# A two-block network in fp32: products without a reader in TensorE's waits, a split gather ahead of the experts, and merged slices in the nets

## The chip, the core and the metric

The kernel runs on one NeuronCore of a Trainium2 chip. Its engines are TensorE (PE; PEld is its weight load), VectorE (DVE), ScalarE (ACT), GpSimd (POOL) and SyncE (SP), which issues most of the DMAs. The metric is the device time of one run in microseconds: the kernel before took 2341.85 us, the median of three runs.

## The reference, cut to what matters

Two blocks follow each other on 256 tokens of width 1024, all in fp32. The first ends in an expert layer in which each of 16 experts takes the 32 tokens with the highest router affinity. The second has two layers, each with two feed-forward nets ("nets" below) of hidden width 2816 around a mixing part.

```python
def expert_choice_moe(h, w_router, w_gate, w_up, w_down):
    affinity = jax.nn.softmax((h @ w_router).astype(jnp.float32), axis=-1)
    gates, idx = lax.top_k(jnp.swapaxes(affinity, 1, 2), cap)      # cap = 32, 16 experts
    xe = h[b_idx, flat_idx].reshape(B, E, cap, D)
    a = jnp.einsum('becd,edf->becf', xe, w_gate)                   # f = 2048
    u = jnp.einsum('becd,edf->becf', xe, w_up)
    ye = jnp.einsum('becf,efd->becd', jax.nn.silu(a) * u, w_down) * gates[..., None]
    return jnp.zeros_like(h).at[b_idx, flat_idx].add(...)

def swiglu_ffn(x, wi, wo):                                         # two per layer, two layers
    g, u = jnp.split(x @ wi, 2, axis=-1)
    return (jax.nn.silu(g) * u) @ wo
```

## The kernel before, in words

Each engine has its own program, and semaphores order them. VectorE and ScalarE finish one operation before the next begins, through the helper in which every one of their instructions is recorded (line 208).

**Split products.** Outside the experts, fp32 values are multiplied in rounded halves. A weight unit (128 rows of 1024 values) is copied rounded by ScalarE (the high part) and its remainder is written by VectorE (the low part). `split_mm` then makes three products into the same PSUM place: high by high, high by low, low by high (line 1910 for the layers, 1624 for the first block). Four unit buffers go round; SyncE fills a ring of six 1 MB slots with weights ahead of them.

**A net** has 22 steps. In step c TensorE makes `up(c + 1)`, which is a gate unit and an up unit of 8 row slices each, and then `down(c)`, which is 12 products of 512 columns. VectorE and ScalarE make the hidden slice of c in between: VectorE multiplies gate and up sums out of PSUM, ScalarE takes the tanh, and VectorE writes the high and low part of the slice (`hid_split`) and splits the next units (`sub`). A loop of five turns holds four steps each, and two steps follow it.

**The experts** stream 192 pieces of 2 MB through eight buffers: three pairs of ring slots, `wide`, three of `moe_ring` and `turned_and_rows`. Piece i goes to buffer i mod 8. SyncE issues the pieces in order, each when its buffer has been used (`big_fill`), and waits besides, for the first eight, until the buffer's earlier contents are dead. An expert uses eight pieces for gate and up and four for down. Experts run in a loop of four groups of four.

**Ahead of the first expert** stands a chain. The output projection ends the mixing part of the first block. POOL meanwhile writes a row of modulation values (`mod_rows`) to DRAM and reads it back broadcast to all partitions; VectorE needs it for the residual and the new norm. TensorE transposes the two token tiles, multiplies them by the router matrix (the logits), transposes the probabilities, and VectorE selects 32 tokens an expert with four rounds of a maximum of eight. One-hot rows are made, and the gather is 32 products of 512 columns for all sixteen experts into all eight PSUM banks; eight copies, eight transposes and the opening of the output sums follow before the first expert's product.

## Time and profile before

| | us |
|---|---|
| median of 3 runs | 2341.85 |
| the runs | 2339.44 to 2343.32 |
| the profiled execution | 2342.55 |
| its span, first to last instruction | 2340.8 |

| engine | busy us | share of the span | instructions |
|---|---|---|---|
| PE | 1896.8 | 81% | 12667 |
| PEld | 1345.1 | 57% | 12667 |
| DVE | 969.1 | 41% | 1348 |
| ACT | 696.4 | 30% | 963 |
| POOL | 42.7 | 2% | 68 |

The DMA engines moved 660.73 MB. The shares are means over stages with different limits: the first block up to some 226 us, the experts up to some 1143 us, and the two layers of the second block behind them. A stage's limit is read from its own rows.

### The profile page before, as it was taken

How to read it: one execution, taken by the hardware profiler on the slowest of the kernel's cores; microseconds unless marked ns; L12 is line 12 of the kernel's file. 1: busy time of each engine (PE TensorE's matmuls, PEld its weight loads, DVE VectorE, ACT ScalarE, POOL GpSimd, SP SyncE). 2: the span in 40 equal slices, each digit the busy share in tenths (PEclk: the TensorE clock that was granted, in tenths of full speed). 3: DMA queues.
4: the chain of work that ended last, by engine and by line, in shares of the span. 5: the costliest groups of instructions: out<-in, count | busy, mean ns of one | idle time of the engine just before them, and what ended most of it. 6: DMA issues, size and time to landing. Idle time of an engine off the chain costs nothing.

```text
span 2340.8 us, 33186 instructions
## 1 busy us (share of the span) xinstructions
PE 1896.8 (81%) x12667; PEld 1345.1 (57%) x12667; DVE 969.1 (41%) x1348; ACT 696.4 (30%) x963; POOL 42.7 (2%) x68
## 2 busy tenths in 40 slices
PE   6896655656555556566699999999999999999999
PEld 4674111111111111111499987799989998879997
DVE  3474000000000000000366677676767667766665
ACT  4342000000000000000344455444454435644444
POOL 0000000000000000000000010000000001000000
PEclk8997787787787777877899999999999999999999
DMA  9767999999999999999846653445546475344552
GB/s 366 247 257 310 429 429 428 428 428 428 428 428 429 428 428 428 428 429 428 303 162 204 219 180 127 162 144 188 188 144 198 163 246 176 127 140 164 182 185 85
DMA packets 174812, 660.73 MB, mean 282 GB/s; under 512 B 10051, under 2 KB 108140, under 8 KB 143732
## 3 DMA queue, kind: packets, MB, share of 16 engines
q1 hardware_dynamic: 171980, 654.12, 72.3%
q10 hardware_dynamic: 2376, 3.03, 0.6%
q0 software_dynamic: 352, 2.11, 0.2%
q8 instruction: 75, 1.23, 0.2%
q14 instruction: 29, 0.24, 0.0%
HBM read 656.60 MB, written 2.64 MB: 282 GB/s over the span
## 4 chain that ended last, share of the span: by engine, by line
PE 53%; DMA 37%; DVE 6%; ACT 2%; issue 2%; ACTq 0%; DVEq 0%; POOL 0%; PEldq 0%; POOLq 0%; SPq 0%; PEld 0%
PE PS L1910 43%; DMA turned_and_rows<-in_w_down_e 12%; DMA turned_and_rows<-in_w_gate_e 12%; DMA turned_and_rows<-in_w_up_e 11%; PE PS L1872 3%; DVE arena L208 2%; DVE units L208 2%; PE PS L1624 2%; DVE hn L208 1%; DMA ring<-in_w_in 1%; PE PS L1892 1%; ACT units L208 1%; DMA ring<-in_w_ada 1%; PE PS L2036 1%; PE PS L1593 0%
## 5 line engine op out<-in xcount | busy, mean ns | idle before, releaser
L208 ACT ACTIVATE units<-ring 128x1024 fp32r<-128x1024 f32 (+2 forms) x416 | 438.1, 1053 | 473.3 <-PE PS L1910 425.7
L208 DVE TENSOR_TENSOR units<-ring,units 128x1024 fp32r<-128x1024 f32 (+2 forms) x416 | 505.8, 1216 | 167.9 <-ACT units L208 140.0
L1910 PE MATMUL PS<-hT_split,units 128*128 128x256 f32 x4416 | 545.4, 283 | 1.7 <-DVE hT_split L208 1.7
L1910 PEld LDWEIGHTS PS<-hT_split,units 128*128 128x128 f32 x4416 | 541.1, 192 | 9.8 <-issue 2.6
L208 DVE SCALAR_TENSOR_TENSOR arena<-arena,PS 128x512 f32<-128x512 f32 (+1 forms) x54 | 41.4, 767 | 798.8 <-ACT arena L208 518.0
L208 ACT ACTIVATE arena<-PS 32x256 f32<-32x256 f32 (+4 forms) x135 | 66.9, 496 | 926.8 <-PE PS L1880 310.6
L1910 PE MATMUL PS<-units,hT_split 128*128 128x512 f32 (+2 forms) x1248 | 286.6, 388 | 5.3 <-DVE units L208 2.8
L1910 PEld LDWEIGHTS PS<-units,hT_split 128*128 128x128 f32 x1248 | 231.6, 190 | 50.6 <-DVE units L208 4.9
L1910 PE MATMUL PS<-units,hid_split 128*128 128x512 f32 x1056 | 255.5, 391 | 0.0
L1910 PEld LDWEIGHTS PS<-units,hid_split 128*128 128x128 f32 x1056 | 192.9, 188 | 36.7
L1872 PE MATMUL PS<-moe_ring,arena 128*32 128x512 f32 x768 | 129.4, 808 | 93.3 <-DMA moe_ring<-in_w_gate_e 55.0
L1872 PE MATMUL PS<-ring,arena 128*32 128x512 f32 x768 | 129.6, 810 | 88.9 <-DMA ring<-in_w_up_e 51.3
L1872 PEld LDWEIGHTS PS<-moe_ring,arena 128*32 128x32 f32 x768 | 25.0, 129 | 193.5 <-DMA moe_ring<-in_w_up_e 69.6
L1872 PEld LDWEIGHTS PS<-ring,arena 128*32 128x32 f32 x768 | 24.9, 130 | 190.1 <-DMA ring<-in_w_up_e 82.4
L1892 PE MATMUL PS<-moe_ring,arena 128*32 128x256 f32 x768 | 72.0, 539 | 37.5 <-DMA moe_ring<-in_w_down_e 34.0
L1892 PE MATMUL PS<-ring,arena 128*32 128x256 f32 x768 | 63.5, 488 | 39.7 <-DMA ring<-in_w_down_e 39.7
L208 ACT ACTIVATE arena<-arena 128x256 f32<-128x256 f32 (+3 forms) x133 | 58.4, 439 | 111.9 <-DVE arena L208 103.2
L208 DVE TENSOR_TENSOR arena<-PS,hn 128x256 f32<-128x256 f32 (+1 forms) x90 | 39.8, 442 | 94.6 <-PE PS L1910 89.8
L1872 PE MATMUL PS<-turned_and_rows,arena 128*32 128x512 f32 x256 | 46.9, 870 | 34.8 <-DMA turned_and_rows<-in_w_gate_e 19.1
L1892 PEld LDWEIGHTS PS<-moe_ring,arena 128*32 128x32 f32 x768 | 30.4, 145 | 75.3 <-DMA moe_ring<-in_w_down_e 41.1
L1872 PE MATMUL PS<-wide,arena 128*32 128x512 f32 x256 | 43.1, 806 | 35.4 <-DMA wide<-in_w_up_e 15.3
L1892 PEld LDWEIGHTS PS<-ring,arena 128*32 128x32 f32 x768 | 27.6, 135 | 76.8 <-DMA ring<-in_w_down_e 55.3
(206 smaller groups left out, 1229.4 us busy)
## 6 DMA issues: line engine op xcount, KB each, us to landing
ring<-in_ffn_wi SPq DMA_DIRECT2D x88, 1024.0 KB, 5.5
ring<-in_w_gate_e SPq DMA_DIRECT2D x24, 2048.0 KB, 36.1
moe_ring<-in_w_up_e SPq DMA_DIRECT2D x24, 2048.0 KB, 35.6
ring<-in_w_down_e SPq DMA_DIRECT2D x24, 2048.0 KB, 35.5
moe_ring<-in_w_gate_e SPq DMA_DIRECT2D x24, 2048.0 KB, 35.5
ring<-in_w_up_e SPq DMA_DIRECT2D x24, 2048.0 KB, 37.0
moe_ring<-in_w_down_e SPq DMA_DIRECT2D x24, 2048.0 KB, 36.9
ring<-in_ffn_wo SPq DMA_DIRECT2D x44, 1024.0 KB, 5.0
```

Of the source, the lines that this page charges most:

```text
L208: return instruction(*args, **kwargs)
L1624: passes = [mm(out, lhs[i], rhs[j], start=start and i + j == 0, stop=stop and i == 1, **flags) for i, j in ((0, 0), (0, 1), (1, 0))]
L1872: last = mm(PS[32 * g:32 * g + 32, 2 + part, :], xe[:, k, :], big(at, 2, SLOT)[:, kk, 512 * g:512 * g + 512], start=(k == 0), stop=(k == K ...
L1892: last = mm(PS[32 * g:32 * g + 32, 5, 0:256], e_hT[:, s, 32 * j:32 * j + 32], big(at, 4, D)[:, s, 256 * g:256 * g + 256], start=(j == 0 an ...
L1910: passes = [mm(out, lhs[i], rhs[j], start=start and i + j == 0, stop=stop and i == 1, **flags) for i, j in ((0, 0), (0, 1), (1, 0))]
L2036: last = mm(PS[:, bank, :], pT[:, j, t * P:(t + 1) * P], w_ple[:, j, 512 * n:512 * n + 512], start=(j == 0), stop=(j == 1))
```

## The change

1. **Products without a reader.** `keep_busy(bank, n)` makes n fp32 products of 128 x 256 into a PSUM bank that nobody reads. They stand before a dozen of TensorE's waits: around the router's transposes and logits, before the selection's transposes, in each group's last expert, and before transposes of the second block.
2. **The gather in two parts.** The one-hot rows and the gather are made for the first four experts first (32 products of 128 columns); VectorE copies the first expert's rows straight out of PSUM, and the first expert begins. The rest (32 products of 384 columns, the copies, the transposes, the opening of the sums) stands between that expert's up and down products. The first group of experts is therefore written out ahead of the loop.
3. **Buffers renumbered.** Pieces 0 to 2 go to the ring pairs and piece 3 to `wide`. The first three pieces wait for ring slots alone.
4. **Selection and copies.** The first maximum reads PSUM, one subtraction is gone (the constant counts from 1), and ScalarE copies the whole first tile's transposes before it squares the second.
5. **Merged slices in the nets.** In 19 of the 22 steps the first two products of a row slice, which share their weights, become one product of 512 columns over both parts of the moving side. The two column halves of the PSUM bank have to be added: VectorE does it with a reduction over pairs. Gate and up take a bank each. Steps 0, 1 and 21 stay as they were, and the loop has four turns.
6. **Order in the mixing parts.** Single operations of VectorE, ScalarE and TensorE are moved against each other.

TensorE between the output projection and the first expert, before (L1815 are the transposes, L1822 the logits, L1827 and L1831 the selection's transposes, L1840 the gather, L1848 and L1853 what follows it):

```order
L1815 MATMUL PS<-cst,hn 128x128 x8
L1822 MATMUL PS<-arena,hT 128x16 x8
L1815 MATMUL PS<-cst,hn 128x128 x8
L1822 MATMUL PS<-arena,hT 128x16 x8
L1827 MATMUL PS<-cst,arena 16x128 x2
L1831 MATMUL PS<-cst,arena 128x16 x2
L1840 MATMUL PS<-onehot_rounded,hn_split 128x512 x32
L1848 MATMUL PS<-cst,arena 128x128 x8
L1853 MATMUL PS<-zeros 128x2 x4
```

And in the change, where L1643 is `keep_busy`, L1880 and L1888 are transposes and logits, L1900 and L1905 the selection's transposes, L1916 the gather and L1968 the expert:

```order
L1643 MATMUL PS<-cst 128x256 x2
L1888 MATMUL PS<-arena,hT 128x16 x8
L1643 MATMUL PS<-cst 128x256 x3
L1880 MATMUL PS<-cst,hn 128x128 x8
L1643 MATMUL PS<-cst 128x256
L1888 MATMUL PS<-arena,hT 128x16 x8
L1643 MATMUL PS<-cst 128x256 x4
L1900 MATMUL PS<-cst,arena 16x128 x2
L1643 MATMUL PS<-cst 128x256 x11
L1905 MATMUL PS<-cst,arena 128x16 x2
L1643 MATMUL PS<-cst 128x256
L1916 MATMUL PS<-onehot_rounded,hn_split 128x128 x32
```

The gather has shrunk from 512 to 128 columns, and L1643 stands before each wait. Behind these rows come 64 products of the first expert, and only then the other part of the gather (128x384 x32).

VectorE in one step of a net, before (`hn` is the row of roots, the `TENSOR_TENSOR units` rows are splits of weight units):

```order
L208 TENSOR_TENSOR arena<-PS,hn 128x256
L208 TENSOR_TENSOR arena<-arena,PS 128x256
L203 REGISTER_ALU
L208 TENSOR_TENSOR units<-ring,units 128x1024
L203 REGISTER_ALU
L208 SCALAR_TENSOR_TENSOR arena<-arena 128x256
L208 CAST hid_split<-arena 128x256
L208 TENSOR_TENSOR hid_split<-arena,hid_split 128x256
L203 REGISTER_ALU
L208 TENSOR_TENSOR units<-ring,units 128x1024
```

And in the change:

```order
L210 TENSOR_REDUCE arena<-PS 128x256
L210 TENSOR_TENSOR arena<-arena,hn 128x256
L205 REGISTER_ALU
L210 TENSOR_TENSOR units<-ring,units 128x1024
L210 TENSOR_REDUCE arena<-PS 128x256
L210 TENSOR_TENSOR arena<-arena 128x256
L205 REGISTER_ALU
L210 SCALAR_TENSOR_TENSOR arena<-arena 128x256
L210 CAST hid_split<-arena 128x256
L210 TENSOR_TENSOR hid_split<-arena,hid_split 128x256
L205 REGISTER_ALU
L210 TENSOR_TENSOR units<-ring,units 128x1024
```

Each of the two products out of PSUM has become a reduction out of PSUM and a product in SBUF, with the down unit's split between the gate and the up half.

VectorE at the branch products of a layer, before (`head_ms` marks the normed rows of one branch, `a_split` its second part, 128x16 the attention's sink):

```order
L208 TENSOR_TENSOR arena<-arena,head_ms 128x1024
L208 TENSOR_TENSOR arena<-arena 128x1024
L208 TENSOR_TENSOR units<-ring,units 128x1024
L208 SCALAR_TENSOR_TENSOR hn<-PS,wide 128x256
L208 SCALAR_TENSOR_TENSOR hn<-PS,wide 128x128
L208 TENSOR_REDUCE arena<-hn 128x1 x2
L208 TENSOR_SCALAR arena<-arena,cur 128x2
L208 TENSOR_TENSOR arena<-arena,cur 128x16
L208 TENSOR_TENSOR a_split<-PS,a_split 128x1024
L208 TENSOR_TENSOR units<-ring,units 128x1024 x4
```

VectorE at the same place in the change:

```order
L210 SCALAR_TENSOR_TENSOR hn<-PS,wide 128x256
L210 SCALAR_TENSOR_TENSOR hn<-PS,wide 128x128
L210 TENSOR_REDUCE arena<-hn 128x1 x2
L210 TENSOR_SCALAR arena<-arena,cur 128x2
L210 TENSOR_TENSOR arena<-arena,head_ms 128x1024
L210 TENSOR_TENSOR arena<-arena 128x1024
L210 TENSOR_TENSOR units<-ring,units 128x1024
L210 TENSOR_TENSOR arena<-arena,cur 128x16
L210 TENSOR_TENSOR units<-ring,units 128x1024 x2
L210 TENSOR_TENSOR a_split<-PS,a_split 128x1024
L210 TENSOR_TENSOR units<-ring,units 128x1024 x2
```

The last head's scores (the rows on `hn<-PS,wide` to 128x2) stand before the normed rows now, and two of the four unit splits before `a_split`.

The diff, cut to its core:

```diff
-            return (POS_LAYER + 2 * (m - 1)) % R
+            return (POS_LAYER + 2 * m) % R

         def big(i, *dims):

             m = i % BIG
-            if m == 0:
+            if m < 3:
+                v = ring[:, ring_pair(m):ring_pair(m) + 2, :].rearrange("p a n -> p (a n)")
+            elif m == 3:
                 v = wide.rearrange("p a n -> p (a n)")
-            elif m < 4:
-                v = ring[:, ring_pair(m):ring_pair(m) + 2, :].rearrange("p a n -> p (a n)")
             elif m < 7:
                 v = moe_ring[:, m - 4, :]
             else:
...
-                if i == 0:
+                if i < 3:
+                    sp.wait_ge(S["slot_used"], POS_LAYER - R + 2 * i + 2)
+                elif i == 3:
                     sp.wait_ge(S["x_mid"], 1)
-                elif i < 4:
-                    sp.wait_ge(S["slot_used"], POS_LAYER - R + 2 * (i - 1) + 2)
                 elif i == 4:
                     sp.wait_ge(S["mixed"], NT)
...
+                if t == 1:
+                    act.wait_ge(S["first_T"], 7)
+                    activation(hT[:, :, 0:P], two_banks(4).rearrange("p (k n) -> p k n", k=KT), ACT.Copy).then_inc(
+                        S["first_hT"], 1)
...
             dve.wait_ge(S["select_T"], 1)
-            dve.run(V.tensor_copy, affT[0:NE, :], PS[0:NE, 1, 0:TOK])
             for i in range(CAP // 8):
-                dve.run(V.max, top8[0:NE, :], affT[0:NE, :])
-                dve.run(V.match_replace, affT[0:NE, :], top8[0:NE, :], affT[0:NE, :], -1.0)
+                left = PS[0:NE, 1, 0:TOK] if i == 0 else affT[0:NE, :]
+                dve.run(V.max, top8[0:NE, :], left)
+                dve.run(V.match_replace, affT[0:NE, :], top8[0:NE, :], left, -1.0)
             ts(chosen[0:NE, :], affT[0:NE, :], -1.0, None, ALU.is_equal)
             dve.run(V.tensor_tensor_scan, count[0:NE, :], chosen[0:NE, :], zeros[0:NE, :], 0.0, ALU.add, ALU.add)
-            tt(count[0:NE, :], count[0:NE, :], chosen[0:NE, :], ALU.mult)
-            ts(affT[0:NE, :], count[0:NE, :], 1.0, None, ALU.subtract).then_inc(S["selected"], 1)
+            tt(affT[0:NE, :], count[0:NE, :], chosen[0:NE, :], ALU.mult).then_inc(S["selected"], 1)
             dve.wait_ge(S["select_T"], 2)
-            for t in range(NT):
-                last = tt(onehot_rounded[:, t, :, :], con("cap_iota").unsqueeze(1).to_broadcast([P, NE, CAP]),
-                   wide_of(PS[:, 2, t * NE:t * NE + NE], CAP), ALU.is_equal)
-            last.then_inc(S["selected"], 1)
+            for first, last_e in ((0, GROUP), (GROUP, NE)):
+                for t in range(NT):
+                    last = tt(onehot_rounded[:, t, first:last_e, :],
+                              con("cap_iota").unsqueeze(1).to_broadcast([P, last_e - first, CAP]),
+                              wide_of(PS[:, 2, t * NE + first:t * NE + last_e], CAP), ALU.is_equal)
+                last.then_inc(S["selected"], 1)
+            for half in range(2):
+                dve.wait_ge(S["gathered"], half + 1)
+                last = dve.run(V.tensor_copy, xe[:, 4 * half:4 * half + 4, :],
+                               PS[:, 6 + half, :].rearrange("p (k n) -> p k n", k=4)[:, :, 0:CAP])
+            last.then_inc(S["xe"], 1)
...
-                def sub(c, hidden, base):
-                    act_, gu = f_act[:, c % 2, :], f_gu[:, c % 2, :]
-                    if c == FFN_SUBS - 1:
-                        down_rest(off, c, base)
-                    dve.wait_ge(S["unit_used"], base + (2 * off + gate_unit(c) + 2))
-                    tt(act_, PS[:, c % 4, 0:TOK], root_row, ALU.mult).then_inc(S["f_gate"], 1)
-                    tt(gu, act_, PS[:, c % 4, TOK:2 * TOK], ALU.mult)
-                    if c < FFN_SUBS - 1:
-                        down_rest(off, c, base)
...
+                    act_, gu = f_act[:, c % 2, :], f_gu[:, c % 2, :]
+                    if c == FFN_SUBS - 1:
+                        down_rest(off, c, base)
+                    gate_bank, up_bank = 2 * (c % 2), 2 * (c % 2) + 1
+                    if c in SPLIT_SUBS:
+                        dve.wait_ge(S["unit_used"], base + (2 * off + gate_unit(c) + 2))
+                        tt(act_, PS[:, gate_bank, 0:TOK], root_row, ALU.mult).then_inc(S["f_gate"], 1)
+                        tt(gu, act_, PS[:, gate_bank, TOK:2 * TOK], ALU.mult)
+                        if c < FFN_SUBS - 1:
+                            down_rest(off, c, base)
+                    else:
+                        dve.wait_ge(S["unit_used"], base + (2 * off + gate_unit(c) + 1))
+                        dve.run(V.reduce_sum, act_, PS[:, gate_bank, :].rearrange("p (i n) -> p n i", i=2), AX.X)
+                        tt(act_, act_, root_row, ALU.mult).then_inc(S["f_gate"], 1)
+                        down_rest(off, c, base)
+                        dve.wait_ge(S["unit_used"], base + (2 * off + gate_unit(c) + 2))
+                        dve.run(V.reduce_sum, gu, PS[:, up_bank, :].rearrange("p (i n) -> p n i", i=2), AX.X)
+                        tt(gu, act_, gu, ALU.mult)
...
+                piece_rest(5, 2, 3)
                 sw_scores(0)
-                piece_rest(5, 2, 3)
...
+                sw_scores(7)
                 dve.wait_ge(S["head_roots"], l + 2)
                 tt(h_a, h_a, wide_of(by_head(head_ms[:, :]), ML_DV), ALU.mult)
                 tt(sq, sq, mo, ALU.mult).then_inc(S["branch"], 1)
                 piece_rest(8, 3, 4)
-
-                sw_scores(7)
                 tt(sw_stat[:, 2, :, :], sw_stat[:, 0, :, :], wide_of(p_("sink"), NT), ALU.add).then_inc(
                     S["sink_arg"], 1)
+                halves_rest(stage_units(OFF_WA, 2, 0, 2), D, before)
                 dve.wait_ge(S["branch_hi"], 2 * l + 1)
                 tt(a_split[:, 1, :, :].rearrange("p k n -> p (k n)"), PS[:, 4:6, :].rearrange("p b n -> p (b n)"),
                    a_split[:, 0, :, :].rearrange("p k n -> p (k n)").bitcast(F32), ALU.subtract).then_inc(
                     S["branch_hT"], 1)
-                halves_rest(stage_units(OFF_WA, 2), D, before)
+                halves_rest(stage_units(OFF_WA, 2, 2), D, before)
...
+                if name == "mixed":
+                    keep_busy(2, 3)
...
+            def keep_busy(bank, n):
+
+                for _ in range(n):
+                    mm(PS[:, bank, 0:TOK], ident, con("causal")[:, 0:TOK], start=True, stop=True)
...
-            for t in range(NT):
+            def moe_turn(t):
+
+                if t == 0:
+                    pe.wait_ge(S["const_full"], 48)
+                    pe.wait_ge(S["x_mid"], 2)
+                    keep_busy(1, 4)
+                else:
+                    keep_busy(1, 3)
                 pe.wait_ge(S["h_moe"], t + 1)
...
+            logits(1).then_inc(S["logits"], 1)
+            keep_busy(3, 4)
             pe.wait_ge(S["selected"], 1)
...
+            keep_busy(3, 11)
             pe.wait_ge(S["selected"], 2)
...
+            keep_busy(3, 1)
...
-                        last = mm(PS[:, k, :], hn_split[:, i, t, k:D:KT],
-                                  onehot_rounded[:, t, :, :].rearrange("p e c -> p (e c)"),
+                        last = mm(out, hn_split[:, i, t, k:D:KT],
+                                  onehot_rounded[:, t, first:last_e, :].rearrange("p e c -> p (e c)"),
                                   start=(t + i == 0), stop=(t + i == NT))
+                return last
+
+            for half in range(2):
+                for k in range(4):
+                    last = gather(PS[:, 6 + half, k * P:(k + 1) * P], 4 * half + k, 0, GROUP)
                 last.then_inc(S["gathered"], 1)
-            pe.wait_ge(S["xeT"], KT)
-            pe.wait_ge(S["selected"], 4)
-            for q in range(NQ):
-                for t in range(NT):
-                    last = nc.tensor.transpose(
-                        PS[:, 4 + q // 2, (q % 2) * TOK + t * P:(q % 2) * TOK + (t + 1) * P],
-                        gated[:, t, GROUP * q:GROUP * q + GROUP, :].rearrange("p e c -> p (e c)"), ident)
-            last.then_inc(S["gathered"], 1)
-            for bank in (0, 1, 6, 7):
-                mm(PS[:, bank, 0:2], zeros[0:1, 0:P], zeros[0:1, 0:2], start=True, stop=False, skip_group_check=True)
...
+            def gather_rest():
+
+                pe.wait_ge(S["selected"], 4)
+                pe.wait_ge(S["xeT"], 1)
+                for k in range(KT):
+                    if k == 4:
+                        pe.wait_ge(S["xeT"], 1 + 4)
+                    gather(PS[:, LATE_BANK[k % 4], 0:NE * CAP - P], k, GROUP, NE).then_inc(S["gathered"], 1)
...
                 fills = q * (GROUP_SLOTS // BIG * 16)
+                alone = isinstance(q, int)
...
+                    if alone and r == 0:
+                        gather_rest()
...
+            experts(0)
+            with pe.Fori(1, NQ) as q:
+                experts(q)
...
-                                first, last = split_mm(PS[:, c % 4, part * TOK:(part + 1) * TOK],
-                                                       [unit(i, n, KT, P)[:, k, :] for i in range(2)],
-                                                       [hT_split[:, i, k, :] for i in range(2)],
-                                                       start=(k == 0), stop=(k == KT - 1))
+                                w = [unit(i, n, KT, P)[:, k, :] for i in range(2)]
+                                if c in SPLIT_SUBS:
+                                    first, last = split_mm(PS[:, 2 * (c % 2), part * TOK:(part + 1) * TOK], w,
+                                                           [hT_split[:, i, k, :] for i in range(2)],
+                                                           start=(k == 0), stop=(k == KT - 1))
+                                else:
+                                    bank = 2 * (c % 2) + part
+                                    first = mm(PS[:, bank, :].rearrange("p (i n) -> p i n", i=2), w[0], hT_split[:, :, k, :],
+                                               start=(k == 0), stop=False, skip_group_check=True)
+                                    last = mm(PS[:, bank, 0:TOK], w[1], hT_split[:, 0, k, :], start=False,
+                                              stop=(k == KT - 1), skip_group_check=True)
...
-                        gate_units(0, 1, 3)
-                        neg_m()
+                        gate_units(0, 1, 2)
+                        neg_m(0)
+                        gate_units(0, 2, 3)
+                        neg_m(1)
```

## Rows read from the trace of the kernel before

**Rows 1.** The span in 40 slices, share of the DMA engines (the page, part 2)

```profile
DMA  9767999999999999999846653445546475344552
```

**Rows 2.** Chain of waits in order of time: start us, us, engine, line, count

```profile
225.94 15.52 PE PS L1872 x128
...
1103.49 35.52 DMA turned_and_rows<-in_w_down_e
...
1162.10 181.44 PE PS L1910 x1272
...
1345.25 1.77 PE PS L1566 x16
...
1348.73 11.51 PE PS L1910 x96
...
1413.08 1.92 PE PS L2129 x8
```

**Rows 3.** Timeline of SyncE's DMA issues: start us, us, line, tensors

```profile
177.27 0.37 SPq L511 DMA_DIRECT2D wide<-in_w_gate_e  x1
...
200.74 0.33 SPq L511 DMA_DIRECT2D turned_and_rows<-in_w_up_e  x1
229.46 0.33 SPq L511 DMA_DIRECT2D wide<-in_w_down_e  x1
```

**Rows 4.** By stretch: busy us of each engine, granted TensorE clock, DMA share, GB/s

```profile
196.00:200.00 4.00, 3.22 (x16) 3.03 (x15) 3.14 (x3) 1.66 (x2) 0.00 (x0) 0.50 1.01 430
```

**Rows 5.** DMA issues of 118 to 140 us: size, us to landing

```profile
arena<-mod_rows POOLq DMA_DIRECT2D x1, 1024.0 KB, 9.2
mod_rows<-wide POOLq DMA_DIRECT2D x1, 8.0 KB, 5.6
```

**Rows 6.** DMA issues of 160 to 200 us: size, us to landing

```profile
arena<-mod_rows POOLq DMA_DIRECT2D x1, 1024.0 KB, 5.0
arena<-in_w_router ACTq DMA_DIRECT2D x1, 64.0 KB, 9.7
mod_rows<-wide POOLq DMA_DIRECT2D x1, 8.0 KB, 1.8
```

**Rows 7.** Timeline from the output projection to the first expert

```profile
164.20 0.64 POOL L617 DMA_DIRECT2D mod_rows<-wide  x1 [13.71 <-DVE wide L208]
...
170.52 2.54 DVE L208 TENSOR_TENSOR units<-ring,units 128x1024 fp32r<-128x1024 f32 x2 [0.20 <-ACT units L208]
...
177.32 1.23 DVE L208 TENSOR_TENSOR hn<-PS,arena 128x1024 f32<-128x1024 f32 x1 [0.34 <-ACT arena L208]
...
196.97 3.60 PE L1822 MATMUL PS<-arena,hT 128*128 128x16 f32 x16 [0.78 <-DVE hT L208]
...
203.32 0.42 DVE L208 MAX8 arena<-arena 16x8 f32<-16x256 f32 x1
...
211.44 9.77 PE L1840 MATMUL PS<-onehot_rounded,hn_split 128*128 128x512 f32 x32 [1.63 <-DVE onehot_rounded L208]
```

**Rows 8.** Timeline of one step of a feed-forward net

```profile
1252.88 2.91 PE L1910 MATMUL PS<-units,hid_split 128*128 128x512 f32 x12
...
1253.08 0.42 DVE L208 TENSOR_TENSOR arena<-PS,hn 128x256 f32<-128x256 f32 x1 [0.56 <-PE PS L1910]
1253.60 0.42 DVE L208 TENSOR_TENSOR arena<-arena,PS 128x256 f32<-128x256 f32 x1
...
1255.63 5.92 PE L1910 MATMUL PS<-hT_split,units 128*128 128x256 f32 x48
...
1257.02 1.22 DVE L208 TENSOR_TENSOR units<-ring,units 128x1024 fp32r<-128x1024 f32 x1 [0.16 <-ACT units L208]
```

**Rows 9.** Groups of instructions by form: busy us, mean ns

```profile
L208 DVE TENSOR_REDUCE arena<-arena 128x2 f32<-128x512 f32 x8 | 5.5, 686 | 0.6
```

**Rows 10.** Timeline at the first layer's branch products, VectorE

```profile
1466.73 1.22 DVE L208 TENSOR_TENSOR a_split<-PS,a_split 128x1024 fp32r<-128x1024 f32 x1 [4.41 <-ACT a_split L208]
```

**Rows 11.** The same stretch, TensorE

```profile
1469.42 5.96 PE L1910 MATMUL PS<-units,a_split 128*128 128x512 f32 x24 [1.83 <-DVE units L208]
```

147 lines of the change are left out of this document (97 added, 50 removed).

## The prediction

> **What bounds the kernel now.** I read the page's slices first, then the chain of waits, then timelines of the places that the change touches. The slices show the DMA engines full from the fifth of the 40 to the nineteenth [rows 1]: that is the expert stage. The chain of waits says the same: from 241 to 1139 us it is loads of expert weights, with TensorE only as links between them; the last lands at 1103.49 + 35.52 = 1139.01 us [rows 2]. SyncE reloads a weight buffer for the first time at 229.46 us [rows 3], and 184 of the 192 loads are still to come then: (1139.01 - 229.46) / 184 = 4.943 us each. So the stage ends 909.55 us after the first reload, whatever TensorE does in it, and only an earlier first reload shortens it. Behind it TensorE bounds: a net is one unbroken piece of 1272 products in 181.44 us [rows 2]. Between two nets VectorE and TensorE alternate, with short waits.
>
> **The nets (12.6 us less).** In before, each row slice of the gate and up products is three products of 256 columns; the change makes it one of 512 and one of 256 for 19 of a net's 22 steps. 96 products of 256 columns take 11.51 us, 119.9 ns each [rows 2]; 12 of 512 columns take 1255.63 - 1252.88 = 2.75 us, 229.2 ns each [rows 8]. Check on the whole piece: 1008 x 119.9 + 264 x 229.2 = 181.4 us, as the row has it. A slice then costs 349.1 instead of 359.7 ns, 10.6 less; I take 10.4, with 119.8 out of the step itself. There are 16 slices x 19 steps x 4 nets = 1216, so 12.6 us. From below: no row has a product whose moving side is two separate pieces; if it costs what its two halves cost, the gain is 0.
> The Trainium skill, "TensorE: Matmul & The Clock Gate", section "Back-to-back issue gap", gives N / 2.4 + 2.5 ns for a warm product. By it a merged slice would save only 2.5 ns, 3.0 us in all. The trace disagrees: 119.9 and 229.2 ns are 13 and 16 ns above N / 2.4, so I keep the rows.
> What hides the edit is VectorE, and it gets tight. A merged step takes one reduction of 512 inputs and one product of 256 for each half. The nearest row for a reduction is 686 ns [rows 9], a 256-wide operation is 0.42 us and the split of a weight unit 1.22 [rows 8]. A step then has 2 x 0.69 + 2 x 0.42 + 1.14 (the three that finish the hidden slice) + 3 x 1.23 = 7.05 us in ten operations, with gaps of 0.1 to 0.16 us between them [rows 8], 1.3 in all: 8.35 us. TensorE's step falls from 8.50 to 8.33 us. So the engines are level. A hidden slice is asked for 5.6 us after the last down product ended, and by this count is ready at 2.4, so there are some 3.2 us to use up over 19 steps: a lag of 0.02 us a step does not reach TensorE. The bound upwards: a reduction that costs 1.23 us (what 1024 elements cost) makes the step 9.43 us, a rival below.
>
> **The way to the first expert (9.5 us earlier).** Three terms.
> First, the loads that now come early. Three ring buffers come first in the new numbering and wait only for ring slots, so the first two go out at some 158.4 and 162.9 us, the third at 174.7, instead of all behind the load into wide at 177.27 [rows 3]. The first two, 4 MB, are then in flight when POOL writes its row at 164.20 [rows 7] and reads it back as 1 MB. On free engines these took 1.8 and 5.0 us [rows 6]; the same pair under loads took 5.6 and 9.2 us [rows 5]. So the write lands at 169.8, and the read, issued 0.3 later and clear of the second load from 172.5 on, at 175 to 178; I take 176.6. VectorE is busy with weight splits until 173.06 [rows 7], then wants the read. Its three following operations had 0.3 us to spare before the one at 177.32, which had waited 0.34 us for ScalarE. That is 3.5 - 0.3 = 3.2 us later for everything behind, between 0.5 and 8 (both transfers at the loaded price).
> The Trainium skill, "DMA: Bandwidth & Descriptors", section "Queues, rings and completion order", says that each DMA engine goes round its queue rows packet by packet. By that a write of 8 KB should lose almost nothing, and the term would be near 1 us. The row shows it 3.8 us later under load, so I keep the larger price.
> Second, the router logits. They end at 196.97 + 3.60 = 200.57 us [rows 7]. ScalarE now copies the first tile's transposes before it squares the second tile, so the first logits need not wait until 190.8. But they need the router matrix, 9.7 us after its issue at 179.95 [rows 6], so not before 189.65; 2 of the added products, each 1.92 / 4 = 0.48 us at the full clock [rows 2] and twice that at half, stand behind that wait and 3 more ahead of the second tile's transposes. The logits themselves took 3.60 us at the granted clock of 0.50 [rows 4, 7] and would take 1.8 at 1.00. The end comes between 6.7 us earlier (matrix early, clock full) and 3.5 later (matrix late, clock at half). I take 1 us earlier, near the late case because the row is for a matrix behind loads, as it will be again.
> Third, from the logits to the first reload: 229.46 - 200.57 = 28.9 us now. New, at the full clock: 1.6 to the probabilities and 0.3 for their transposes; the selection 202.8 to 209.4, 6.5 us, less a copy of 0.42 + 0.07 and a subtraction of 0.36, so 5.7; 0.4 for the next transposes; 0.8 for the one-hot rows of four experts instead of sixteen; 32 products of 128 columns at the price of a transpose, 1.77 / 16 = 0.11, so 3.6 us where 32 of 512 took 9.77 and eight copies, eight transposes and the sums followed; 0.6 for the copy of two small pieces; 1.7 for the first buffer's 16 products, (15.52 - 3.5) / 7 [rows 2], instead of 3.5. Sum 14.7, with semaphores 15.2. The 11 added products of 5.3 us just fit in the 5.7 of the selection, and the 4 before (1.9) stick out by 0.3. At the half clock they take 10.6 and 3.8, and all the rest of TensorE's doubles: 26.7 us. I take 17.2, since TensorE is now busy nearly all along but starts from 0.50, so 11.7 us less.
> Sum: 3.2 - 1 - 11.7 = 9.5 us earlier, between 19 earlier and 2 later.
> What was left out of the way, the gather for the other twelve experts (32 products of 384 columns, about 5.7 us, eight transposes, eight copies), now stands between the first expert's up and down products. Behind it wait the down products, and for them the buffers: the first reload begins after 1.7 us of the first expert, eight take 39.5, and the down products begin about 26 us after the start. So the queue never runs dry, and it costs nothing. The 2 products before late loads in each group's last expert sit in waits of 3 us for a load. The 4 ahead of the last sum are 1.9 us against ScalarE's 1.7: 0.2 later.
>
> **The branches of a layer (3.4 us less).** VectorE waited 4.41 us and then wrote the branch's second part before the weight units; TensorE stood 1.83 us for a unit [rows 10, 11]. Now two units come first, inside that wait, and the last head's scores come earlier, which takes 0.6 us off a wait. The third and fourth unit then come last, so of 2.4 us I count 1.3, and 0.4 for the score piece moved behind a unit: 1.7 a layer, twice. Bounds 0 and 5.
> Heads and units reordered in the first block move nothing: TensorE had its half of the units, and the moved exponentials are wanted 10 us later.
>
> **Sum.** The profiled execution took 2342.55 us (span 2340.8). 2342.55 - 12.6 - 9.5 - 3.4 + 0.2 = 2317.3; the median of the runs, 2341.85, is 0.7 lower, so 2316.5 us, 1.1% less.
>
> **Rivals.**
> 1. The way to the expert gains nothing: the added products run at the half clock, hold up logits and selection, and the broadcast comes late. For: TensorE was granted 0.50 in 196 to 200 us though it worked 3.22 of 4 us [rows 4]. Against: in before it then stood idle. 2316.5 + 9.5 = 2326 us.
> 2. The way is clear: matrix early, full clock, broadcast on time: 19 earlier, 2307 us. For: the first big loads are fewer when the router matrix is asked for. Against: both loaded prices of rows 5.
> 3. VectorE becomes the bound in the nets, the slower side. Place: the two reductions out of PSUM, whose two inputs stand 256 columns apart. Price: at 1.23 us each 19 x (9.43 - 8.33) - 3.2 = 17.7 us a net against the forecast, 71 in all: 2387 us. A net gains nothing from about 0.85 us a reduction, the kernel gets slower from about 0.95. For: no row has a reduction of pairs. Against: 512 and 1024 elements cost the same per element in every form shown.
> 4. The merge saves nothing, products of 512 in two pieces costing 2 x 119.8: 2329 us. By the figure of the Trainium skill cited above it would be 2326.
>
> **How the numbers follow.** Forecast 0.57 (2310 to 2323); rival 1 0.17; rival 2 0.10; rival 3 0.09, of which 0.07 is beyond no change; rival 4 0.07. The range 2303 to 2331 us holds the forecast, rivals 1, 2 and 4 and leaves out rival 3 and tails. About 0.2% is what a measurement of this kernel can tell from none: faster 0.88, within it 0.05, slower 0.07.
>
> **What would show it.** Right: 96 slices' products and 24 down products alternate without idle time of TensorE, a net's piece of about 178.3 us instead of 181.4; VectorE's reductions at 0.69 us; the first reload at 216 to 224 us; the last load 909 to 910 us later; the wait at the branch products at most 0.6 us. Wrong: TensorE waiting for hid_split inside a net (rival 3); a granted clock of 0.5 in the selection (rival 1); mod_rows landing before 173 us; a gap in the DMA share between the first reload and the end of the experts, which would mean that the late gather does hold the buffers.

## Result: 2323.9 us, 0.8% faster, 7.4 us short of the forecast

The changed kernel took 2323.91 us (median of 4 runs, 2320.16 to 2325.17) beside 2342.11 us of the kernel before on the same chip (4 runs): ratio 0.9921, 95% interval 0.9904 to 0.9938. It is faster, inside the forecast's range, but 0.9 us above the 2310 to 2323 us of its likeliest case. The profiled execution took 2324.62 us, its span is 2322.8 us, 18.0 less than before's.

I set the same instants of the two traces beside each other. All places are in the chain of waits of either kernel.

| stretch | before, us | after, us | gain | forecast |
|---|---|---|---|---|
| start to the first reload | 229.46 | 227.59 | 1.9 | 9.5 |
| first reload to the last load's landing | 909.55 | 909.36 | 0.2 | 0 |
| landing to the first net's first products | 15.68 | 17.31 | -1.6 | -0.2 |
| four nets, first products to the next part | 772.96 | 764.40 | 8.6 | 12.6 |
| two mixing parts, from their first 96 products (of 256 columns) to the next net | 354.93 | 345.94 | 9.0 | 3.4 |
| sum, before rounding | | | 18.0 | 25.3 |

The chain of waits of the kernel after (start, us, what) shows the ends of these stretches; they answer to [rows 2]:

```profile
182.86 9.91 DMA arena<-in_w_router
...
215.59 7.93 PE PS L1916 x32
...
1099.73 37.22 DMA turned_and_rows<-in_w_down_e
...
1154.26 5.98 PE PS L2015 x48
...
1192.76 2.75 PE PS L2015 x12
...
1318.57 2.75 PE PS L2015 x12
...
1346.17 11.51 PE PS L2015 x96
```

The last load lands at 1099.73 + 37.22 = 1136.95 us. New in the chain is a DMA ahead of the logits, that of the router matrix. Behind it the 32 products of the short gather (L1916) take 7.93 us, which I had put at 3.6.

**The way to the first expert** in the timeline of the kernel after (start, us, engine, line, operation, names, shapes, count, and in brackets the idle time before with what ended it), answering to [rows 3, 7]:

```profile
157.15 16.92 SPq L513 DMA_DIRECT2D ring<-in_w_gate_e  x3
...
162.70 0.64 POOL L619 DMA_DIRECT2D mod_rows<-wide  x1 [13.72 <-DVE wide L210]
...
176.31 1.23 DVE L210 TENSOR_TENSOR arena<-arena,wide 128x1024 f32<-128x1024 f32 x1 [4.75 <-DMA arena<-mod_rows]
...
180.23 1.22 DVE L210 TENSOR_TENSOR hn<-PS,arena 128x1024 f32<-128x1024 f32 x1
...
192.81 2.08 PE L1643 MATMUL PS<-cst 128*128 128x256 f32 x4 [4.94 <-DMA arena<-in_w_router]
...
208.71 0.42 DVE L210 MAX8 arena<-PS 16x8 f32<-16x256 f32 x1 [1.83 <-PE PS L1900]
...
223.89 4.50 PE L1968 MATMUL PS<-ring,arena 128*32 128x512 f32 x20 [0.38 <-DVE arena L210]
...
227.59 0.33 SPq L513 DMA_DIRECT2D ring<-in_w_down_e  x1
```

The early loads leave from 157.15 us on; the row's write of 8 KB, issued at 162.70, keeps POOL waiting 5.64 us, up to 168.97, where it had been some 1.4, and VectorE waits 4.75 us for the broadcast, which it had not done before. TensorE waits 4.94 us for the router matrix, and its granted clock is 0.50 from 188 to 200 us. VectorE's selection can only start at 208.71.

The instant at which POOL writes the row differs from one profiled execution to the next (160.9 to 164.1 us in 13 profiles of kernels with the changed first block, 164.20 before), so in what follows I measure the way from there to the first reload: 65.26 us before, 64.89 after. The six profiles in which nothing of this way differs from the changed kernel (its own and those of experiments 2, 3, 5, 6 and 7) have 62.9 to 65.2, 64.0 on the mean. So the way as such got 0.4 us shorter in this trace and 1.3 on the mean, not 9.5. The other 1.5 us lie ahead of it; of the kernel before there is one profile, so whether the change won them is open.

**The nets.** Groups by line between 1165 and 1340 us (busy us and mean ns of one, then the idle time before them), answering to [rows 9]:

```profile
L2103 PE MATMUL PS<-hT_split,units 128*128 128x512 f32 x304 | 108.1, 398 | 0.0
L2105 PE MATMUL PS<-hT_split,units 128*128 128x256 f32 x304 | 85.3, 281 | 0.0
...
L210 DVE TENSOR_REDUCE arena<-PS 128x256 f32<-128x512 f32 x38 | 26.3, 692 | 5.8 <-issue 3.2 <-PE PS L2105 0.5 <-PE PS L2015 0.2
```

and three products in a row of the timeline:

```profile
1250.25 0.40 PE L2103 MATMUL PS<-hT_split,units 128*128 128x512 f32 x1
...
1250.48 0.28 PE L2105 MATMUL PS<-hT_split,units 128*128 128x256 f32 x1
...
1250.60 0.40 PE L2103 MATMUL PS<-hT_split,units 128*128 128x512 f32 x1
```

No idle time of TensorE stands in the net (the unbroken piece is 179.3 us long, where it was 181.4 and 178.3 were forecast), and a reduction takes 692 ns, as forecast. The merged product of 512 columns follows its partner by 0.12 us and is followed after 0.23 to 0.24. In the chain above, the down products (L2015, 12 in 2.75 us) of two steps 15 apart begin 1318.57 - 1192.76 = 125.81 us apart: 8.387 us a step, and (8.387 - 2.745) / 16 = 352.6 ns a slice. Forecast: 8.33 and 349.1.

**The mixing part** of the first layer, TensorE's timeline, answering to [rows 11]:

```profile
1467.82 3.08 PE L2015 MATMUL PS<-units,a_split 128*128 128x512 f32 x12 [1.21 <-DVE units L210]
```

and the 96 products behind the norm in the chain of waits, first of the kernel before, then after:

```profile
1498.72 23.64 PE PS L1910 x96
```

```profile
1494.10 22.06 PE PS L2015 x96
```

The branch's first product runs at once (before it waited 1.83 us), the wait is now 1.21 us and later. The 96 products take 22.06 us where they took 23.64, which I had not looked at: it is 1.6 us of the 3.6 won in this part. The granted clock was 0.60 in the first 4 us of them before (1498 to 1502 us) and is 1.00 now.

### The profile page after: what moved, and what is told of

Its sections match the earlier page's. It is cut to its first block, busy times and chain, and to the rows that moved or that the text cites. A ratio compares the mean times of both kernels' runs of the same rounds, so it can differ in the third digit from the quotient of the medians.

```text
span 2322.8 us, 31262 instructions
## 1 busy us (share of the span) xinstructions
PE 1915.0 (82%) x11625; PEld 1306.3 (56%) x11625; DVE 1073.7 (46%) x1500; ACT 697.6 (30%) x965; POOL 43.3 (2%) x68
## 4 chain that ended last, share of the span: by engine, by line
PE 56%; DMA 37%; DVE 4%; ACT 2%; issue 1%; ACTq 0%; DVEq 0%; PEldq 0%; SPq 0%; PEld 0%
PE PS L2015 26%; DMA turned_and_rows<-in_w_down_e 13%; PE PS L2103 12%; DMA turned_and_rows<-in_w_up_e 11%; DMA turned_and_rows<-in_w_gate_e 11%; PE PS L2105 6%; PE PS L1968 3%; DVE arena L210 2%; PE PS L1990 1%; PE PS L1682 1%; DVE units L210 1%; DMA ring<-in_w_in 1%; PE PS L1916 1%; ACT units L210 1%; DMA ring<-in_w_ada 1%
## 5 line engine op out<-in xcount | busy, mean ns | idle before, releaser
L2103 PE MATMUL PS<-hT_split,units 128*128 128x512 f32 x1216 | 432.4, 398 | 0.0
L210 ACT ACTIVATE arena<-PS 128x512 f32<-128x512 f32 (+3 forms) x137 | 67.6, 493 | 923.1 <-PE PS L1976 318.4
L2105 PE MATMUL PS<-hT_split,units 128*128 128x256 f32 x1216 | 341.3, 281 | 0.0
L2015 PE MATMUL PS<-units,hT_split 128*128 128x512 f32 (+2 forms) x1248 | 283.6, 385 | 4.5 <-DVE hT_split L210 2.4
L2103 PEld LDWEIGHTS PS<-hT_split,units 128*128 128x128 f32 x1216 | 228.5, 188 | 55.9
L2015 PEld LDWEIGHTS PS<-units,hT_split 128*128 128x128 f32 x1248 | 229.4, 188 | 48.9 <-issue 4.4
L2015 PE MATMUL PS<-units,hid_split 128*128 128x512 f32 x1056 | 255.4, 391 | 0.0
L2105 PEld LDWEIGHTS PS<-hT_split,units 128*128 128x128 f32 x1216 | 229.6, 189 | 3.0
L2015 PEld LDWEIGHTS PS<-units,hid_split 128*128 128x128 f32 x1056 | 192.2, 188 | 40.4 <-DVE hid_split L210 0.2
L1968 PE MATMUL PS<-moe_ring,arena 128*32 128x512 f32 x768 | 133.7, 835 | 84.8 <-DMA moe_ring<-in_w_up_e 43.8
L1968 PE MATMUL PS<-ring,arena 128*32 128x512 f32 x768 | 132.1, 828 | 85.2 <-DMA ring<-in_w_up_e 51.8
L1968 PEld LDWEIGHTS PS<-moe_ring,arena 128*32 128x32 f32 x768 | 25.4, 133 | 187.1 <-DMA moe_ring<-in_w_up_e 73.5
L1968 PEld LDWEIGHTS PS<-ring,arena 128*32 128x32 f32 x768 | 25.3, 133 | 185.9 <-DMA ring<-in_w_up_e 83.7
L210 DVE TENSOR_REDUCE arena<-PS 128x256 f32<-128x512 f32 (+1 forms) x153 | 105.4, 689 | 24.1 <-PE PS L2105 7.5
L2015 PE MATMUL PS<-hT_split,units 128*128 128x256 f32 x768 | 95.8, 285 | 2.9 <-DVE hT_split L210 2.9
L2015 PEld LDWEIGHTS PS<-hT_split,units 128*128 128x128 f32 x768 | 93.3, 191 | 4.9 <-issue 2.6
L1990 PE MATMUL PS<-moe_ring,arena 128*32 128x256 f32 x768 | 62.3, 480 | 34.1 <-DMA moe_ring<-in_w_down_e 31.3
## 6 DMA issues: line engine op xcount, KB each, us to landing
ring<-in_w_up_e SPq DMA_DIRECT2D x24, 2048.0 KB, 36.4
```

The lines of the kernel that those rows point to most:

```text
L210: return instruction(*args, **kwargs)
L1968: last = mm(PS[32 * g:32 * g + 32, 2 + part, :], xe[:, k, :], big(at, 2, SLOT)[:, kk, 512 * g:512 * g + 512], start=(k == 0), stop=(k == K ...
L1990: last = mm(PS[32 * g:32 * g + 32, 5, 0:256], e_hT[:, s, 32 * j:32 * j + 32], big(at, 4, D)[:, s, 256 * g:256 * g + 256], start=(j == 0 an ...
L2015: passes = [mm(out, lhs[i], rhs[j], start=start and i + j == 0, stop=stop and i == 1, **flags) for i, j in ((0, 0), (0, 1), (1, 0))]
L2103: first = mm(PS[:, bank, :].rearrange("p (i n) -> p i n", i=2), w[0], hT_split[:, :, k, :], start=(k == 0), stop=False, skip_group_check=True)
L2105: last = mm(PS[:, bank, 0:TOK], w[1], hT_split[:, 0, k, :], start=False, stop=(k == KT - 1), skip_group_check=True)
```

## Experiments

All were timed beside the kernel before; each ratio is to that kernel, and the changed kernel's is 0.9921. The intervals are all about 0.0015 to either side, 3.5 us, so single microseconds are read from the traces. "Way" is the time from the row's write to the first reload (after: 64.89 us, 64.0 on the mean).

**1. No products without a reader.**

```diff
             def keep_busy(bank, n):
-                for _ in range(n):
-                    mm(PS[:, bank, 0:TOK], ident, con("causal")[:, 0:TOK], start=True, stop=True)
+                return
```

> The changed kernel without any of the products that nobody reads; all else as changed. Theory A (the products pay, by keeping the granted clock up): the first reload of an expert buffer comes later than 227.6 us, up to 232, with the 16 products of the logits and the 32 of the gather at 3.4 to 3.6 and 7.9 us or more, and in each layer the 96 products of 512 columns behind the mixing part's norm take 23.6 us instead of 22.05, so the whole is 3 to 7 us slower than the changed kernel: some 2327 to 2331 us. Rival B (they cost more than they give): between the router matrix's landing and the selection 4 + 6 + 8 of their instructions stand in the way for 2.1 + 2.9 + 1.2 us, so the first reload comes 4 to 6 us earlier (222 to 224 us) and the whole is 2318 to 2322 us even with the 1.6 us a layer lost. Rival C (the clock does not depend on them): logits, gather and the 96 products as in the changed kernel, first reload 3 to 5 us earlier, the whole 2319 to 2321 us.

Ratio 0.9917 (0.9900 to 0.9933). The way took 60.42 us, 3.5 less than the mean. TensorE after the router matrix's landing:

```profile
191.19 3.59 PE L1887 MATMUL PS<-arena,hT 128*128 128x16 f32 x16 [3.89 <-DMA arena<-in_w_router]
...
210.19 7.91 PE L1915 MATMUL PS<-onehot_rounded,hn_split 128*128 128x128 f32 x32 [0.83 <-DVE onehot_rounded L210]
```

The first tile's logits run at the lower clock (3.59 us for 16 products, as in the kernel before), and yet the logits end 39.3 us after the row's write instead of 42.3, because nothing stands before them. The gather takes 7.91 us without the products, all of it at a clock of 0.50, and 7.92 with them. What they cost here they gave back at the end of the experts:

```profile
1137.36 6.64 PE PS L2001 x8
...
1151.19 8.50 PE PS L2014 x48
```

The sum over experts took 6.64 us instead of 3.70 and the first net's first products 8.50 instead of 5.98, both at the lower clock. Rival B holds for the way; for the whole the two nearly cancel. (The profiled execution took 2324.0 us, 4.3 above the median of 2319.7, so it shows more lost at that end than the usual one.) The 96 products behind the mixing part's norm took 22.02 us here as well, which neither theory had.

**2. Slices of the nets as before.**

```diff
-SPLIT_SUBS = (0, 1, FFN_SUBS - 1)
+SPLIT_SUBS = tuple(range(FFN_SUBS))
```

> The changed kernel with the slices of the nets as before: three products of 256 columns for each, in all 22 steps. Theory A (TensorE sets the pace of a net and the merge is worth the 0.11 to 0.12 us a step that the two traces differ by): a net's step 8.50 us again, each net 2.1 to 2.2 us longer, the whole 8.5 us slower than the changed kernel, some 2332.5 us. Rival B (half of those 2.1 us come from the four steps' new place outside the loop or from other moves): the step at 8.50 but each net only 1 us longer, 2328 us. Rival C (VectorE holds the merged form back, and the split one has something new to gain): not slower, 2324 us or less.

Ratio 0.9960 (0.9948 to 0.9973). The second net took 1711.27 - 1518.89 = 192.38 us from its first products to the next part's, as in the kernel before, instead of 190.26. Theory A: the merge alone is the 2.1 us of a net.

**3. The two halves of the moving side next to each other.**

```diff
-        hT_split = nc.alloc_sbuf_tensor_at("hT_split", [P, 2, KT, TOK], ROUNDED, ...
+        hT_split = nc.alloc_sbuf_tensor_at("hT_split", [P, KT, 2, TOK], ROUNDED, ...
-    first = mm(PS[:, bank, :].rearrange("p (i n) -> p i n", i=2), w[0], hT_split[:, :, k, :],
+    first = mm(PS[:, bank, :], w[0], hT_split[:, k, :, :].rearrange("p i n -> p (i n)"),
```

> The changed kernel with the two halves of the nets' moving side laid next to each other in SBUF (the split activations as k, half, column instead of half, k, column), so that the merged product reads 512 adjacent columns; the same instructions otherwise. Theory A (the two separate pieces cost: a merged product and its partner take 353 ns a slice where 229.2 + 119.8 = 349.0 were forecast): the slice comes to 349 ns, a step to 8.33 us, each net 1.1 us shorter, the whole 4.3 us faster than the changed kernel, 2319.6 us. Rival B (what costs is changing the product's length every time, or the weights' load behind it): the slice stays at 353 ns and the whole at 2324 us. Rival C (VectorE sets the pace at 8.39 us): TensorE's products shorter, but with waits for the hidden slices, the whole at 2324 us.

Ratio 0.9922 (0.9909 to 0.9936); the second net 190.27 us, as with two pieces. Theory A falls: the two pieces cost nothing.

**4. The loads behind the modulation rows.**

```diff
+                if i == 0:
+                    sp.wait_ge(S["mod_full"], 32)
-                elif i == 3:
+                if i == 3:
```

> The changed kernel with one wait more: the first load of expert weights, and so all of them, goes out only when the broadcast of the modulation rows has landed. Theory A (those loads make the row's way out and back slow: 6.0 + 7.3 us where free engines took 1.8 + 5.0): the two take 7 us together, VectorE does not wait 4.75 us for them, the product at 180.2 us comes at 176 to 177, the first reload 3.5 us earlier, at 224 us, and the whole 2320.5 us. The eight loads then start at some 169.5 us and have all landed by 210. Rival B (the router matrix, asked for behind more loads, or the half clock takes the time back): the modulation lands early but the first reload stays at 227 to 228 us, 2324 us. Rival C (the loads themselves become late, and the first expert waits for them): first reload 229 or later, slower than the changed kernel.

Ratio 0.9900 (0.9886 to 0.9913); the way 57.26 us, 6.7 less than the mean, the first reload at 218.54.

```profile
161.28 0.64 POOL L621 DMA_DIRECT2D mod_rows<-wide  x1 [13.71 <-DVE wide L210]
...
174.38 1.23 DVE L210 TENSOR_TENSOR hn<-PS,arena 128x1024 f32<-128x1024 f32 x1 [0.34 <-ACT arena L210]
...
186.58 0.86 PEld L1645 LDWEIGHTS PS<-cst 128*128 128x128 f32 x4 [4.75 <-DMA arena<-in_w_router]
...
207.04 7.91 PE L1918 MATMUL PS<-onehot_rounded,hn_split 128*128 128x128 f32 x32 [0.21 <-DVE onehot_rounded L210]
```

The write is back after 1.40 us of POOL's waiting and the broadcast has landed before VectorE asks. The product that was at 180.23 comes at 174.38. Theory A, and nearly double its size: 4.4 us are the product's, and behind it the clock stood at 1.00 from 194 us to the selection's end, where it had been 0.50 up to 201 us and again from 205 to 208, so that the added products before the selection no longer stuck out. The router matrix still keeps TensorE waiting (4.56 us). And the gather takes 7.91 us again, at a clock of 0.50 from 0.6 us after its start. These are the rows of windows (us, their sum, busy us of PE and of its weight loads, of DVE, ACT and POOL, granted clock, DMA share, GB/s):

```profile
200.00:204.00 4.00, 4.00 (x21) 3.54 (x20) 3.33 (x12) 0.00 (x0) 0.00 (x0) 1.00 0.99 422
...
208.00:212.00 4.00, 4.00 (x18) 4.00 (x18) 0.46 (x2) 0.00 (x0) 0.00 (x0) 0.50 0.24 102
```

**5. The nets' merged slices in fours** (four products of 512 columns, then four of 256).

```diff
-                                    last = mm(PS[:, bank, 0:TOK], w[1], hT_split[:, 0, k, :], start=False,
-                                              stop=(k == KT - 1), skip_group_check=True)
+                                    if k % 4 == 3:
+                                        for kk in range(k - 3, k + 1):
+                                            last = mm(PS[:, bank, 0:TOK], unit(1, n, KT, P)[:, kk, :], hT_split[:, 0, kk, :], ...
```

> The changed kernel with the nets' merged slices in fours: four products of 512 columns, then four of 256, instead of one and one; the same products otherwise. Theory A (a change of length costs TensorE some 2 ns each time, which makes a slice 352.6 ns where 229.2 + 119.8 = 349.0 were forecast): a step 8.34 us instead of 8.39, each net 0.8 to 1.1 us shorter, the whole 3 to 4 us faster than the changed kernel (ratio to before 0.9907 instead of 0.9921). Rival B (VectorE sets the pace of the step): TensorE then waits for hidden slices, and a net stays at 190.3 us from its first products to the next part. Rival C (the 256-wide product cannot be shorter here because its weights load behind a 512-wide one): no change either, but without waits of TensorE.

Ratio 0.9903 (0.9888 to 0.9918); the second net 1706.14 - 1516.49 = 189.65 us, 0.6 less. The chain of waits inside a net:

```profile
1244.55 0.47 PE PS L2107 x4
1245.02 0.93 PE PS L2103 x4
...
1249.23 2.77 PE PS L2015 x12
...
1257.58 2.77 PE PS L2015 x12
```

(0.93 + 0.47) / 4 = 350 ns a slice, 1257.58 - 1249.23 = 8.35 us a step. Theory A in kind, and less in size: 0.6 us over 304 slices are 2.0 of the 3.5 ns by which a slice was too dear. That it is the change of length, and not something else in the new order, is argued and not shown.

**6. VectorE relieved of one reduction a step.**

```diff
-    dve.run(V.reduce_sum, gu, PS[:, up_bank, :].rearrange("p (i n) -> p n i", i=2), AX.X)
-    tt(gu, act_, gu, ALU.mult)
+    tt(gu, act_, PS[:, up_bank, 0:TOK], ALU.mult)
```

> The changed kernel in which VectorE does not add the two halves of the up product (it multiplies by the first half alone: the correction by the second one is left out of the result, for all merged steps): one reduction of 0.69 us and its gap of about 0.1 less a step for VectorE. Theory A (TensorE sets the pace): a net as in the changed kernel, 190.3 us from its first products to the next part, step 8.39. Rival B (VectorE sets it): the step falls to 8.33 us, each net 1.1 us shorter.

Ratio 0.9911 (0.9896 to 0.9926); the second net 1703.88 - 1513.65 = 190.23 us, the same. TensorE sets the pace; VectorE's share of the step is covered.

**7. VectorE's order at the branches as before.**

```diff
-                sw_scores(7)
                 dve.wait_ge(S["head_roots"], l + 2)
...
                 piece_rest(8, 3, 4)
+                sw_scores(7)
...
-                halves_rest(stage_units(OFF_WA, 2, 0, 2), D, before)
                 dve.wait_ge(S["branch_hi"], 2 * l + 1)
```

> The changed kernel with the order of VectorE at the branches of a layer as before (the last head's scores behind the gating, the branch's second part ahead of the two weight units); the products without a reader stay. The traces differ by 3.6 and 5.35 us in the two mixing parts: 0.2 ahead of the branch, 1.9 to 3.6 in it, and 1.6 in the 96 products behind the norm, which took 23.63 us before and 22.05 now. Theory A (the order takes the waits away, and the waits were what let the granted clock fall): 1.9 us a layer for the waits and 1.6 for the 96 products come back, so both mixing parts are 3 to 5 us longer, the whole 6 to 9 us slower than the changed kernel, ratio to before 0.995 to 0.996. Rival B (the order is worth only the waits; the clock is kept by the added products): 22.05 us for the 96 products, the whole 3.5 to 4 us slower, ratio 0.9937.

Ratio 0.9929 (0.9915 to 0.9942). From a net's first products to the 96 products of the mixing part 1497.55 - 1156.20 = 341.35 us instead of 339.84, and 341.58 instead of 339.95 in the second layer: 1.5 and 1.6 us. The 96 products kept 22.02 us. Rival B's reading, that the added products hold the clock, was not enough either, since experiment 1 had none.

**8. The early gather for eight experts**, 32 products of 256 columns instead of 128.

```diff
-    for k in range(4):
-        last = gather(PS[:, 6 + half, k * P:(k + 1) * P], 4 * half + k, 0, GROUP)
+    for k in range(4):
+        last = gather(PS[:, 6 * half + k // 2, (k % 2) * 2 * P:(k % 2 + 1) * 2 * P], 4 * half + k, 0, 2 * GROUP)
```

> The changed kernel with the early part of the gather for eight experts instead of four: 32 products of 256 columns, and the late part 256 instead of 384. The early one took 7.92 us for 128 columns, 247 ns a product, at a granted clock of 0.50. Theory A (at that clock the loading of the 128 weights sets the pace, so columns up to 256 are free, 213 ns at 1.2 GHz): the early part 7.9 us again, the late one 1 us shorter where nothing waits for it, the first reload 0 to 1 us later for longer copies, the whole equal. Theory B (the clock falls because products of 128 columns leave the array idle while weights load): with 256 columns the clock stays up, the early part takes 4 to 5 us, the first expert starts at the full clock, and the first reload comes 4 to 5.5 us earlier, the whole 2319 us, ratio 0.990. Rival C: time goes with the columns, 10 us or more, and the kernel is slower by 3 us.

Ratio 0.9905 (0.9890 to 0.9920); the way 62.69 us, 1.3 less.

```profile
213.35 7.94 PE L1916 MATMUL PS<-onehot_rounded,hn_split 128*128 128x256 f32 x32 [0.47 <-DVE onehot_rounded L210]
...
221.68 0.16 PEld L1968 LDWEIGHTS PS<-ring,arena 128*32 128x32 f32 x8 [0.58 <-DVE arena L210]
...
223.66 0.33 SPq L513 DMA_DIRECT2D ring<-in_w_down_e  x1
```

```profile
216.00:220.00 4.00, 4.00 (x19) 4.00 (x18) 0.29 (x1) 0.00 (x0) 0.00 (x0) 1.00 0.00 0
```

The clock stays at 1.00 through the whole gather, and the first expert's first buffer is free 1.98 us after its start instead of 3.70. (Why it stays is not shown: in experiment 9, with as many columns, it fell.) But the 32 products take 7.94 us at the full clock with twice the columns. So 248 ns is the price of neither the clock nor the columns, and neither theory had that.

The trace of the changed kernel already held this. Its late gather makes the same products with 384 columns at the full clock:

```profile
240.26 4.22 PE L1916 MATMUL PS<-onehot_rounded,hn_split 128*128 128x384 f32 x16
```

```profile
240.00:244.00 4.00, 4.00 (x19) 3.74 (x16) 0.56 (x1) 0.94 (x2) 0.00 (x0) 1.00 0.99 426
```

The copies that follow each four of them start 0.97 us apart (242.58, 243.55, 244.52), 243 ns a product. And the early gather ran at 1.00 in its first 3.2 us and at 0.50 behind them without a change of pace.

**9. Weights of the gather adjacent** (on top of experiment 8). They are the rows' split, taken every eighth element; here they are stored so that 128 in a row make a product's weights. In this run and in number 11 VectorE, by its operands in the trace, still read and wrote 1024 adjacent elements. So it took the rounded part of one element from the value of another, and the second part of the split is not what the reference asks; the two runs tell of times alone.

```diff
-            activation(hn_split[:, 0, 1, :], hn[:, 1, :], ACT.Copy).then_inc(S["hn_hi"], 1)
+            activation(by_k(hn_split[:, 0, 1, :]), by_row(hn[:, 1, :]), ACT.Copy).then_inc(S["hn_hi"], 1)
-                        last = mm(out, hn_split[:, i, t, k:D:KT],
+                        last = mm(out, hn_split[:, i, t, k * P:(k + 1) * P],
```

> The changed kernel with the early gather for eight experts, as in the run before, and with the split rows that are its weights stored so that the 128 columns of a product are adjacent (they stood 8 elements apart); the same products and sizes. Measured so far: 247 ns a product at the granted clock 0.50 with 128 columns and 247 to 248 ns at 1.00 with 256. Theory A (neither clock nor columns set that pace, but the loading of weights that stand 32 bytes apart): the 32 products take 3.8 us at the full clock (119.8 ns each) instead of 7.94, the first reload comes 4 us earlier than in that run, the whole 2315 to 2316 us, ratio to before 0.989. Rival B (it is the one-hot matrix or two banks being written by turns): 7.9 us again and nothing gained. Rival C (VectorE and ScalarE write the rows 128 elements apart and are slow at it): 1 to 3 us lost on the way, above all the rows' second part, which stands behind the logits.

Ratio 0.9901 (0.9886 to 0.9917); the way 60.68 us, 2.0 less than in experiment 8.

```profile
203.81 1.97 ACT L210 ACTIVATE hn_split<-hn 128x1024 fp32r<-128x1024 f32 x1
...
216.31 5.56 PE L1918 MATMUL PS<-onehot_rounded,hn_split 128*128 128x256 f32 x32 [0.47 <-DVE onehot_rounded L210]
```

```profile
216.00:220.00 4.00, 3.69 (x19) 3.72 (x20) 1.30 (x4) 0.00 (x0) 0.00 (x0) 0.61 0.00 0
```

5.56 us, with the clock at 0.61 in the first four. The second 16 products took 221.91 - 219.64 = 2.27 us between the two copies that follow each half, 142 ns each on the mean; the clock came back to 1.00 only at 220.3 us. Theory A for the mechanism; ScalarE pays 1.97 instead of 1.06 us for writing 128 elements apart (rival C), and the clock was the worse one here.

**10. Neither the products nor the new order at the branches** (the edits of 1 and 7).

> The changed kernel without any product nobody reads and with VectorE's order at the branches of a layer as before. With either alone undone the 96 products behind the mixing part's norm still took 22.02 us (23.63 in the kernel before). Theory A (the wait at the second transposes and the waits of the branch together let the clock fall; removing one kind is enough to hold it): 23.6 us again in both layers, and the mixing parts 3.2 us longer than in the changed kernel. Rival B (something else holds it, the split of the two rows of minus m or the merged nets): 22.0 us, and the mixing parts 1.6 us longer. For the way to the first expert both expect what the run without products showed: first reload 5 to 6 us before the changed kernel's; at the end of the experts 18.8 us from the last load to the next net instead of 15.6; the whole 2325 us with A, 2322 with B.

Ratio 0.9934 (0.9920 to 0.9947). The mixing parts' 96 products:

```profile
1491.12 23.62 PE L2014 MATMUL PS<-units,hT_split 128*128 128x512 f32 x96 [0.34 <-DVE hT_split L210]
```

```profile
2078.41 23.53 PE L2014 MATMUL PS<-units,hT_split 128*128 128x512 f32 x96 [0.35 <-DVE hT_split L210]
```

Theory A: with both undone, 23.62 us again, as before. Either of the two edits is enough to hold the clock, and the order saves 1.5 us of waits besides (1491.12 - 1147.18 is 343.94 us against 339.84, of which 2.6 are the first net's slower first products).

**11. Together**: experiments 4, 5, 8 and 9, and the router matrix asked for before ScalarE's last halves of the first block.

```diff
+            program.dma_start(w_router, a["w_router"][0].rearrange("(p k) e -> p k e", k=KT)).then_inc(
+                S["router_full"], 16)
             first_hi(28, 29, 30, 31)
```

> The changed kernel with the loads of expert weights behind the modulation rows, the router matrix asked for some 12 us earlier (ahead of ScalarE's last four halves, when no expert load is in flight yet), the early gather for eight experts from adjacent weights, and the nets' slices in fours. Theory A (the terms add up): against the changed kernel's first reload of 227.6 us, 9 us less for the loads, 6 less for the logits (4.6 of them the wait for the router matrix, the rest the clock), 4 to 5.5 less for the gather and the first buffer, so 208 to 210 us; from there the DMA engines have no idle time any more, because eight loads of 4.94 us from 168.2 us on last until 207.8. Nets 0.6 us shorter each. The whole some 2320 - 19 - 2.4 + 0: 2300 us, ratio to before 0.983. Rival B (the loads now are the bound: the first expert waits for the sixth to eighth buffer, and the first reload is not earlier than 213): 2304 to 2305 us, ratio 0.985. Rival C (the router matrix, asked for beside the modulation rows, delays them): first reload 218 as without it, 2311 us.

Ratio 0.9834 (0.9821 to 0.9848), 2302.78 us beside 2340.89; the way 46.13 us, the first reload at 208.06.

```profile
163.24 0.33 ACTq L772 DMA_DIRECT2D arena<-in_w_router  x1
...
183.53 1.96 PE L1891 MATMUL PS<-arena,hT 128*128 128x16 f32 x16 [0.25 <-ACT hT L210]
...
201.63 4.06 PE L1919 MATMUL PS<-onehot_rounded,hn_split 128*128 128x256 f32 x32 [0.47 <-DVE onehot_rounded L210]
...
208.06 0.33 SPq L517 DMA_DIRECT2D ring<-in_w_down_e  x1
```

```profile
204.00:208.00 4.00, 3.61 (x35) 2.16 (x37) 1.78 (x4) 1.88 (x2) 0.00 (x0) 1.00 1.03 442
```

The logits follow the copies at once, the clock stays at 1.00, the gather's 32 products take 4.06 us (127 ns each), and the DMA share is 0.97 to 1.05 in each 4 us up to the first reload. Theory A: 208.06 us where it had 208 to 210, and the whole 2.8 us above its 2300.

**12. The same with both parts of the rows in the new order**, with the maximum ahead of VectorE's second subtraction, and the first load behind the row's write only.

```diff
-                    sp.wait_ge(S["mod_full"], 32)
+                    sp.wait_ge(S["mod_written"], 32)
```

> The kernel of all parts together, now with both parts of the split rows stored by their products (in the run before VectorE still wrote the second, small part in the old order, which is cheaper than writing it 128 elements apart: that part of the result was left wrong); the maximum of the logits stands ahead of the rows' second subtraction on VectorE, and the first load of expert weights waits only for the modulation rows' write, not for their broadcast. Before these changes: first reload 208.06 us, DMA engines without idle time from 169 us, selection from 194.50 us, gather 4.06 us. Theory A: VectorE's strided write costs it nothing (1.23 us as ScalarE's went from 1.06 to 1.97: at most 2.1), the selection starts 1 us earlier, the loads begin at 164 instead of 169 us, first reload 206 to 208 us, the whole 2300 to 2303 us. Rival B: the broadcast beside the loads takes 7.3 us again and its rows come 0.5 to 2 us too late for VectorE, which eats the gain: first reload 208 to 210, 2303 to 2305 us. Rival C: VectorE's strided write takes over 2.5 us and holds up the gather: 210 or later.

Ratio 0.9865 (0.9848 to 0.9881), 2307.99 us beside 2338.58: faster than both kernels, but the way took 50.98 us, 4.9 more than in experiment 11.

```profile
163.18 9.28 SPq L517 DMA_DIRECT2D ring<-in_w_gate_e  x3
...
174.26 1.23 DVE L210 TENSOR_TENSOR arena<-arena,wide 128x1024 f32<-128x1024 f32 x1 [4.30 <-DMA arena<-mod_rows]
...
195.58 1.94 DVE L210 TENSOR_TENSOR hn_split<-hn,hn_split 128x1024 fp32r<-128x1024 f32 x1
```

Rival B, larger than I had put it: the broadcast takes 11.1 us from its issue to its landing beside the loads, not 7.3, and VectorE waits 4.30 us for it. VectorE's subtraction, now reading one operand and writing 128 elements apart, takes 1.94 to 2.01 us instead of 1.23. The gather takes 4.06 us here too, with the right values. The load's wait on the broadcast was the better one. It was not run with the rest of this kernel.

## Why the forecast was right in sign and 7.4 us too low

**In sum.** The time fell inside the range partly by luck. The nets and the way gave 4.0 and 7.6 us less than forecast, and the branches gave 5.6 more by something that the forecast did not have; without that the kernel would have come out at 2329.5 us, near the range's upper end.

**Right.** Expert stage: 909.36 us behind the first reload, and the DMA share is 1.01 from 260 to 1000 us, so the late gather holds up nothing. Nets: TensorE never waits in them and a reduction takes 692 ns, so rival 3 is out (experiment 6 shows that VectorE has slack), and rival 4 is out by experiment 2.

**The nets, 8.6 instead of 12.6.** The failed term is the slice: "a slice then costs 349.1 instead of 359.7 ns", which is 229.2 + 119.9 out of runs of equal products. Alternated they take 352.6. That the moving side is in two pieces, the doubt I had named, costs nothing (3); in fours, with fewer changes of length, they take 2.0 ns less (5). By the Trainium skill, "TensorE: Matmul & The Clock Gate", section "Back-to-back issue gap", whose formula is for a single product, the merge would have been worth an estimated 2.5 ns a slice; the traces have 359.7 - 352.6 = 7.1, between that and the 10.6 of the forecast.

**The way to the first expert, 1.9 instead of 9.5.** All three terms failed, the first two by size, the third by mechanism. I count them from the row's write.
First term: "that is 3.5 - 0.3 = 3.2 us later". The product moved from 13.1 to 17.5 us behind the write: 4.4 later. Experiment 4 confirms the cause. The write took 6.0 instead of 1.8 us beside the loads, so the row was the right witness. By the Trainium skill, "DMA: Bandwidth & Descriptors", section "Queues, rings and completion order", each DMA engine serves its queue rows in turn, packet by packet; that a small write would then lose almost nothing was my conclusion from it, and these numbers disagree.
Second term: "I take 1 us earlier". The logits ended at 42.3 instead of 36.4 us, so 1.5 later beyond the first term. The router matrix took 9.9 us, as forecast, and is asked for 4.4 us later behind the write, as the first term has it. Ten of the instructions without a reader then stand in TensorE's queue, at half clock, ahead of the logits and the second transposes (2.1 + 2.9 us); experiment 1 without them ends the logits 2.9 us earlier. I had named 3.5 us later as the bound for a late matrix and the half clock, and chose 1 us earlier without working it out.
Third term: from the logits to the reload 22.6 us, against 28.9 before; I took 17.2, and 15.2 at the full clock. The 7.4 us above 15.2 are, but for rounding, 4.3 of the gather, 2.0 of the first buffer at the half clock (3.70 instead of 1.7), and 1.2 of the products ahead of the selection, half-clocked too (3.48 us instead of 1.9). The step that failed is "32 products of 128 columns at the price of a transpose, 1.77 / 16 = 0.11". The transposes are fp32 and the gather is fp32r; the weights of both stand 8 elements apart, but only the gather pays for it, and why the transposes do not was not tried. The rows of the kernel before could hardly show it. I had put all of the 305 ns a product of [rows 7], beside the 229.2 of [rows 8], down to the clock, and most of it was: in that trace the products start 427 ns apart at 0.50 and 245 at 1.00. With 512 columns only the last 16 ns are not the clock's. Experiments 1, 8 and 9 separate the causes: 247 ns at 0.50 with 128 columns and 248 at 1.00 with 256, but 127 ns at 1.00 with adjacent weights (11, 12), and 174 in experiment 9, most of it at 0.50.
Rival 1 had this outcome, and its half clock, held-up logits and late broadcast all came; the gather's price it did not have. Experiment 8 shows that the full clock there gives back 1.7 us, in the first buffer, and nothing in the gather.

**The branches, 9.0 instead of 3.4.** "1.7 a layer" for VectorE's order measured 1.5 and 1.6 (experiment 7), though the wait is still 1.21 us where I had named 0.6 at most. The step that failed is that the branches' term held waits alone. Half of the rest stood in a row that I did not open: the 96 products behind the norm, 23.64 us in the kernel before and 22.0 in every other stretch of this kind, 1.6 a layer. The clock fell behind the waits of the branch and of the norm; with the order changed, or with products in the norm's wait, it does not (1, 7, 10). In the second layer before, 24 products of the branch were slow as well, 7.39 us where the first layer has 5.96. With the old order experiments 7 and 10 have 5.95 in both layers, so these 1.4 us belong to the one execution and not to the change. Some 1.3 of the 9.0 us stay unassigned.

**The end of the experts.** It lost 1.6 us in the profiled execution: its last down products took 3.56 us at a low clock, which in experiments 2, 3, 4, 6, 8 and 9 took 1.93, and the stretch then was 15.7 us as before. In 5, 7, 11 and 12 the stretch was 17.1 to 17.3 us, though 6 and 7 are the same kernel up to there. So this is a chance of the clock, not of the change. Without the products it was 18.8 us once (1) and 15.7 once (10), with 8.5 and 8.6 us for the net's first products. Beside these two runs the products save 2.5 us in the net's first products. But the kernel before had none either, and its one profile has 15.7 and 5.99 us: beside it they gained nothing. I had priced them at -0.2.

**Open.** Where the other 1.5 ns of a slice go; why the clock stays up in some gathers and falls in others; whether the kernel before would lose clock at the end of the experts in other executions; why the row's write comes up to 3.2 us sooner or later from one execution to the next, which may have decided 1.5 of the 1.9 us; and whether the loads behind the broadcast, with both parts of the rows stored as in experiment 12, reach 2303 us.

## What to carry to other kernels

Price a product by its stationary side too: look for a row with the same type and the same distance between the weights' elements, not only with the same columns, before calling a slow one a matter of the clock. An early transfer is not free: list the small transfers that are then in flight on the path (here a row's round trip, 4.4 us on the path, and the router matrix, 9.9 us instead of 1.7) and let the large ones wait for them, or ask for the small ones first. Work that only keeps the clock up belongs where the engine is known to wait longer than it lasts, at the half clock too.

## What the runs showed of the hardware

- fp32r products whose 128 weights stand 8 elements apart: 247 ns with 128 columns at a granted clock of 0.50 (7.91 us for 32, experiment 1), 248 with 256 at 1.00 (8), 243 with 384 at 1.00 (the changed kernel's late gather), 245 with 512 at 1.00 (the kernel before); from adjacent weights 127 ns with 256 columns at 1.00 (11, 12). fp32 transposes with weights 8 elements apart do not pay for it (16 in 1.77 us, 111 ns each).
- Equal products of 512 and of 256 columns take 229.2 and 119.9 ns; alternating, the pair takes 352.6; in fours 350 to 351.
- A moving side in two pieces 2048 elements apart costs the same as one piece (190.26 and 190.27 us a net).
- Writing 1024 elements a partition 128 elements apart: ScalarE 1.96 to 2.01 us instead of 1.06; VectorE, with one operand read 128 apart as well, 1.94 to 2.01 instead of 1.23 (12).
- 8 KB written and read back as 1 MB beside 2 MB loads: 6.0 and 7.3 us; alone 1.7 and 4.6; the read-back issued together with the loads 11.1 us (12). 64 KB behind four such loads: 9.9 us; before them 1.7.
- The granted clock fell to 0.50 during the 32 gather products of 128 columns in all seven profiles that entered them at 1.00, 0.6 us after their start in experiment 4 and 3.9 in 5. With 256 columns it held in 8, 11 and 12 and fell 0.6 us after the start in 9.
